# First block: the next stage starts from the un-normalised residual, and layer norm is applied to its results

## What is computed

```python
h = layer_norm(h, ln_in_g, ln_in_b)
for l in range(2):
    h = layer_norm(ALPHA * h + 0.5 * swiglu_ffn(h, ffn1...), ln_g[l,0], ln_b[l,0])
    mix = token_mix(h, ...)   # z = h @ w_in; pool, conv, retention; @ w_out
    h = layer_norm(ALPHA * h + mix, ln_g[l,1], ln_b[l,1])
    h = layer_norm(ALPHA * h + 0.5 * swiglu_ffn(h, ffn2...), ln_g[l,2], ln_b[l,2])
# layer_norm(x) = (x - mean) * rsqrt(var + eps) * g + b, over the 1024 features
```

## Time and profile before

| | |
|---|---|
| median of 3 runs | 1942.44 us (1942.26 to 1943.13) |
| span of the profiled execution | 1940.9 us |
| PE, PE weight load busy | 1769.2 us (91%), 1687.4 us (87%) |
| DVE, ACT, POOL busy | 1137.7, 816.8, 228.1 us |
| chain that ended last, by engine | PE 82%, DVE 9%, ACT 5%, issue 3% |

### The profile page before, as it was taken

How to read it: one execution, slowest core, us unless ns; L and a number is a source line. 1 busy time by engine, 2 the same in 40 slices (tenths; PEclk the granted TensorE clock), 3 DMA queues, 4 the chain that set the end, 5 groups by cost and what they waited for, 6 DMA issues and landing times.

```text
span 1940.9 us, 33661 instructions
## 1 busy us (share of the span) xinstructions
PE 1769.2 (91%) x13290; PEld 1687.4 (87%) x13290; DVE 1137.7 (59%) x1492; ACT 816.8 (42%) x1072; POOL 228.1 (12%) x258
## 2 busy tenths in 40 slices
PE   6999988889998999978889997899799978679998
PEld 5999987689998999978589996898799977579997
DVE  5555477665555555478665545566666456465654
ACT  4333353353334333254343334574434336543432
POOL 1000047000000000038010000130000001300000
PEclk9999999899999999999899999998899989789999
DMA  4545423134453445423144453242355523035552
GB/s 171 180 174 196 142 107 131 44 126 174 175 188 126 163 173 202 154 89 132 49 157 173 173 208 117 87 142 93 118 180 197 193 88 119 22 109 175 193 201 81
DMA packets 37096, 277.72 MB, mean 143 GB/s; under 512 B 4289, under 2 KB 4417, under 8 KB 6801
## 3 DMA queue, kind: packets, MB, share of 16 engines
q1 hardware_dynamic: 35872, 271.73, 39.6%
q0 software_dynamic: 1136, 4.83, 0.7%
HBM read 275.49 MB, written 1.05 MB: 142 GB/s over the span
## 4 chain that ended last, share of the span: by engine, by line
PE 82%; DVE 9%; ACT 5%; issue 3%; POOL 0%; DMA 0%; DVEq 0%; SPq 0%; ACTq 0%; POOLq 0%
PE bank L562 25%; PE bank L564 25%; PE bank L563 25%; PE bank L580 3%; DVE w_lo L1419 2%; DVE rstd L1427 1%; ACT w_hi L1015 1%; DVE conv_y L1580 1%; DVE o_rstd L1655 1%; DVE y L1439 1%; ACT h L1042 0%; ACT att_p L1221 0%; PE bank L823 0%; PE bank L849 0%; DMA ident<-in_ident 0%
## 5 line engine op out<-in xcount | busy, mean ns | idle before, releaser
L562 PE MATMUL bank<-h_hi,w_hi 128*128 128x272 f32 (+1 forms) x2624 | 763.3, 291 | 55.0 <-DVE h_lo L1443 26.7
L564 PE MATMUL bank<-h_hi,w_lo 128*128 128x272 f32 (+1 forms) x2624 | 760.7, 290 | 0.0
L563 PE MATMUL bank<-h_lo,w_hi 128*128 128x272 f32 (+1 forms) x2624 | 758.8, 289 | 0.0
L1419 DVE TENSOR_TENSOR w_lo<-raw,w_hi 128x2048 fp32r<-128x2048 f32 (+2 forms) x242 | 589.9, 2438 | 251.7 <-ACT w_hi L1015 250.3
L1015 ACT ACTIVATE w_hi<-raw 128x2048 fp32r<-128x2048 f32 (+2 forms) x241 | 486.2, 2018 | 221.3 <-PE bank L564 215.4
L562 PEld LDWEIGHTS bank<-h_hi,w_hi 128*128 128x128 f32 x2624 | 504.3, 192 | 61.5 <-issue 50.1
L564 PEld LDWEIGHTS bank<-h_hi,w_lo 128*128 128x128 f32 x2624 | 504.1, 192 | 0.0
L563 PEld LDWEIGHTS bank<-h_lo,w_hi 128*128 128x128 f32 x2624 | 503.9, 192 | 0.0
L562 PE MATMUL bank<-g_hi,w_hi 128*128 128x272 f32 (+1 forms) x1344 | 390.7, 291 | 7.7 <-DVE g_lo L1531 3.8
L564 PE MATMUL bank<-g_hi,w_lo 128*128 128x272 f32 (+1 forms) x1344 | 386.4, 287 | 0.0
L563 PE MATMUL bank<-g_lo,w_hi 128*128 128x272 f32 (+1 forms) x1344 | 385.6, 287 | 0.0
(11 more groups left out here) (249 smaller groups left out, 1411.1 us busy)
## 6 DMA issues: line engine op xcount, KB each, us to landing
raw<-in_up_w SPq DMA_DIRECT2D x132, 1024.0 KB, 4.7
raw<-in_down_w SPq DMA_DIRECT2D x48, 1408.0 KB, 6.0
raw<-in_in_w SPq DMA_DIRECT2D x20, 1024.0 KB, 4.7
raw<-in_out_w SPq DMA_DIRECT2D x16, 1024.0 KB, 4.8
raw<-in_even_w SPq DMA_DIRECT2D x12, 1024.0 KB, 4.8
raw<-in_odd_w SPq DMA_DIRECT2D x6, 1024.0 KB, 4.7
raw<-in_in_w SPq DMA_DIRECT2D x4, 512.0 KB, 3.4
decay<-in_decay POOLq DMA_DIRECT2D x1, 1632.0 KB, 10.9
```

The source lines that it names most:

```text
L562: pe.matmul(out, w[0], x[0], start=first, stop=False)
L563: pe.matmul(out, w[0], x[1], start=False, stop=False)
L564: return pe.matmul(out, w[1], x[0], start=False, stop=last)
L1419: dve.tensor_tensor(w_lo[:, slot, 0:blocks * P], raw[:, slot, 0:blocks * P], w_hi[:, slot, 0:blocks * P].bitcast(F32), ALU.subtract).then_ ...
```

## The change

**Five of the six layer norms of the first block are deferred** (all but the last, `LAST_NORM`). With r the residual tile, a constant per token m0 (the mean of tile 0) taken off it, and g, b the norm's gain and bias, the next stage's first chunks (4 up chunks, `DEFER_UP`, or 3 in-projection chunks, `DEFER_IN`) are multiplied from `u = g * r`, split as `u_hi`, `u_lo`. Two columns of u (274 instead of 272) hold -g and b, so that PE's result has -W g and W b beside it. DVE then turns a finished bank into `(bank + mu * (-Wg)) * rstd` (`deferred_norm`); the bias W b is added by ACT's silu or copy or by DVE. Meanwhile POOL normalises the residual itself in eight passes of 544 elements (`normalise`), ACT makes `h_hi` and `h`, DVE `h_lo`, and the chunks from `DEFER_UP` or `DEFER_IN` on use these as before.

**The statistics** come from two running sums on POOL, of y and of its squares (`residual_sums`), with one matmul by ones for each; variance is the mean square less the squared mean. POOL also takes m0 off the 7 or 6 tiles of `h` that are still to be added. The factor ALPHA is moved into the branch (`BRANCH_FFN`, `BRANCH_MIX`).

**The input norm** is taken token-wise on `x_tok` before the transposes (`bn_stats`), the constants' DMAs wait for x, and weight chunk 0 is loaded and split in two halves. **Order:** in the in-projection the pooling tiles come third (`IN_ORDER`), so `pool_windows` stands after the three deferred chunks; the first two taps on DVE stand later. The layer loop is written out twice.

The core of the diff (lines starting with a space are unchanged):

```diff
+IN_ORDER = [2, 3, 4, 5, 0, 1] + list(range(6, 22))
+BRANCH_FFN, BRANCH_MIX = 0.5 / ALPHA, 1.0 / ALPHA
+U = T + 2
+DEFER_UP, DEFER_IN = 4, 3
...
 # POOL
+            def residual_sums(taken):
+                pool.wait_ge(affine, seen.next(affine, KD))
+                pool.wait_ge(m0_copied, seen.next(m0_copied))
+                for k in range(taken, KD):
+                    pool.tensor_tensor(h[:, k, :], h[:, k, :], m0[:], ALU.subtract).then_inc(hm_ready, 1)
+                for k in range(1, KD):
...
+                    pool.tensor_tensor(acc[:], acc[:] if k > 1 else y[:, 0, :], y[:, k, :], ALU.add)\
...
+                    pool.tensor_tensor(acc2[:], acc2[:] if k > 1 else sqb[:, 0, :], sqb[:, k % 2, :], ALU.add)\
...
+            def normalise():
+                pool.wait_ge(u_ready, seen.next(u_ready, KD))
+                pool.wait_ge(mu_ready, seen.next(mu_ready))
+                pairs = [y[:, 2 * j:2 * j + 2, :] for j in range(KD // 2)]
+                for p in pairs:
+                    pool.tensor_tensor(p, p, both_tiles(mu), ALU.subtract).then_inc(t1_ready, 1)
+                pool.wait_ge(rstd_ready, seen.next(rstd_ready))
+                for p in pairs:
+                    pool.wait_ge(t1_ready, seen.next(t1_ready))
+                    pool.tensor_tensor(p, p, both_tiles(rstd), ALU.mult).then_inc(t_ready, 1)
...
 # PE
+            def shifted_tile(bank, slot, tiles, e, first):
+                for k in range(KD):
+                    if first:
+                        pe.wait_ge(u_ready, seen.next(u_ready))
+                    last = mm3(bank[:, 0:U], wpair(slot, k * tiles + e), upair(k), k == 0, k == KD - 1)
+                if first:
+                    residual_sums()
+                return last
...
 # ACT
+            def shifted_tile(l, i, k):
+                act.wait_ge(y_ready, seen.next(y_ready))
...
+                    act.activation(us(u_hi, k, 0, T), y[:, k, :], ACT.Identity, scale=vcol(l, V_LN + 16 * i + k))\
...
+                if k >= 2:
+                    act.wait_ge(acc2_added, seen.at(acc2_added, max(1, k - 2)))
+                act.activation(sqb[:, k % 2, :], y[:, k, :], ACT.Square).then_inc(squared, 1)
...
 # DVE
+            def residual_deviation():
+                dve.wait_ge(mean_ready, seen.next(mean_ready))
+                dve.tensor_scalar(mu[:], ps[6][:, 0:T], 1.0 / D, None, ALU.mult).then_inc(mu_ready, 1)
...
+            def deferred_norm(c, q, w, banks, free):
+                dve.wait_ge(chunk_used, st.value(c, 0, 2))
+                for e in range(2):
+                    last = dve.tensor_copy(wgb[:, w + e, :], banks[e][:, T:T + 2])
+                link(last)
+                for e in range(2):
+                    last = dve.scalar_tensor_tensor(q[:, e, :], mu[:], wgb[:, w + e, 0:1], banks[e][:, 0:T],
+                                                    ALU.mult, ALU.add)
...
+                dve.tensor_tensor(q, q, both_tiles(rstd), ALU.mult).then_inc(q_ready, 1)
...
+                def first_chunks():
+                    take(0)
+                    split_next(UP_BLOCKS, 0, 2)
+                    gated(0)
+                    take(1)
+                    split_next(UP_BLOCKS, 0, 3)
+                    low_tile(0)
...
+                    gated(1)
+                    take(2)
...
 # in-projection, DVE
-                    if c == 1:
-                        pool_windows()
...
+                take(0)
+                split_next(2 * KD, 0, 2)
+                take(1)
+                split_next(2 * KD, 0, 3)
...
+                dve.tensor_tensor(upad[:, :, TAPS - 1:], ca[:], cg[:], ALU.mult).then_inc(conv_in, 1)
+                for k in range(5):
+                    low_tile(k)
+                take(2)
+                split_next(2 * KD, 0, 4)
...
+                pool_windows()
```

More of the change, by code:

```diff
@@ L134, in region, with pairs_of @@
     return take
-def pairs_of(eng, n, step):
-    for j in range(2):
-        step(0, j, False)
-    with eng.Fori(1, n // 2 - 1) as i:
+def pairs_of(eng, n, step, done=2):
+    for c in range(done):
+        step(c // 2, c % 2, False)
+    with eng.Fori(done // 2, n // 2 - 1) as i:
         for j in range(2):
@@ L200, in forward @@
         spans = ((ghi_at + KD * T4, glo_at), (glo_at + KD * T4, g_end), (rest_at, limit))
-        one = placer(region(*spans))
+        late = placer(region((rest_at, limit)))
+        v_tok = late("v_tok", [P, 3, HEADS * P])
+        gate_s = late("gate_s", [P, HEADS, T])
+        o_c = late("o_c", [P, HEADS, T])
+        o_rstd = late("o_rstd", [P, HEADS, T])
+        late_end = rest_at + (3 * HEADS * P + 3 * HEADS * T) * 4
+        u_hi = place("u_hi", [P, KD * U], F32R, rest_at)
+        u_lo = place("u_lo", [P, KD * U], F32R, rest_at + KD * U * 4)
+        assert 2 * KD * U * 4 <= late_end - rest_at
+        one = placer(region((ghi_at + KD * T4, glo_at), (glo_at + KD * T4, g_end), (late_end, limit)))
         xpad = one("xpad", [P, 2, 16 + T])
@@ new lines, in forward @@
+        xstd_ready = sem("xstd_ready")
+        xscale_ready = sem("xscale_ready")
+        xn_ready = [sem(f"xn_ready{i}") for i in range(3)]
+        xT_ready = sem("xT_ready")
+        y_ready = sem("y_ready")
+        y0_ready = sem("y0_ready")
+        m0_ready = sem("m0_ready")
+        m0_copied = sem("m0_copied")
+        hm_ready = sem("hm_ready")
+        gb_done = sem("gb_done")
+        u_hi_done = sem("u_hi_done")
+        u_ready = sem("u_ready")
+        squared = sem("squared")
@@ L445, in ffn @@
                     src = a[name].rearrange("f c p n -> (f c) p n")
-                    with sp.Fori(0, n // 2) as c:
+                    ahead = 0
+                    if i == 0 and name == "up_w":
+                        half = UP_BLOCKS // 2 * P
+                        sp.dma_start(raw[:, 0, 0:half], src[0, :, 0:half]).then_inc(half_loaded, 16)
+                        sp.dma_start(raw[:, 0, half:2 * half], src[0, :, half:2 * half]).then_inc(loaded[0], 16)
+                        load(src[1], blocks, 1)
+                        ahead = 1
+                    with sp.Fori(ahead, n // 2) as c:
                         for j in range(2):
@@ L626, in down @@
                                    k == 0, k == FT - 1)
+                        if n == T and isinstance(i, int) and (i, j, k) == (0, 1, 3):
+                            shift()
                     last.then_inc(chunk_used, 1)
-                up(0, 0)
-                up(0, 1)
-                with pe.Fori(1, FT // 2) as i:
+                for c in range(shifted + 2):
+                    up(c // 2, c % 2, c)
+                with pe.Fori(shifted // 2 + 1, FT // 2) as i:
                     up(i, 0)
@@ L1556, in _ @@
+            for l in range(LAYERS):
+                ffn(IN_GROUPS[0] * KD, T, l, 0, l > 0)
+                split_next(IN_GROUPS[1] * KD, 0, 1)
+                residual_deviation()
                 dve.memset(xpad[:, :, 0:16], 0.0)
```

801 lines of the change are left out of this document (522 added, 279 removed).

## The result

The changed kernel runs in 1917.68 us (median of 4 runs, 1917.24 to 1924.63) beside 1942.79 us of the kernel before on the same chip: a ratio of 0.988 (95% interval 0.986 to 0.989). The forecast was 1908. The profiled execution has a span of 1915.4 us, 25.5 less than before, where 34 were forecast. All executions compared in this document are fast ones, except one of the four of b2 (3368.79 us), which its ratio leaves out.

A forecast was written before the change was run, and what follows sets the result against it. PE, with 82% of the chain of waits, was taken as the bound, so time is won only where it stands still. Terms -15 - 6.5 - 6 - 3 - 3.5 = -34 from 1942.4 gave 1908 us; range 1890 to 1927.

The forecast's parts named there:

- rivals 1 and 4: POOL and DVE exclude each other in full (1930 or 1924), or all five norms gain zero (1924); together 0.26.
- rival 1: POOL and DVE exclude each other in full: 1930 at all poor ends, else 1924; 0.26 shared with the zero-gain case.
- The start: Input norm and first chunk: chunk 0 starts at 20 to 21 us, -15 us (ends -13.5, -16.5).
- The norm behind the second feed-forward: Deferred norm in layer 0: 7.0 us lost where 13.5 were, so -6.5 us (ends -4.9, -8.9).
- The walk without POOL: Deferred norm before a feed-forward, POOL's passes left out: chunk 4 at 28.7 against 24.1 us, 4.6 us lost.
- the rows say less than in full: 0.1 us more: Deferred norm: DVE's two-input operation takes 537 ns beside the convolution, 442 elsewhere, so 7.0 us lost, not 8.6.
- The two out-projections: Norms behind them: 10.5 us lost where 13.5 were, -3 us each, -6 together (ends +1.8, -15.6).
- POOL comes late: Behind the out-projections: POOL's 20 operations, 17 us, start only 14.5 us before the last product.
- at no cost: Extra columns, down-stage drains, weight loads, constants and the written-out layer loop were said to cost nothing.
- In-projections: DVE bounds both: -6.7 to +3.6 us each, taken as -1.5 each, -3 together.
- The last norm: Not deferred, new statistics: squares at 16.3 us after the last product instead of 20.0, -3.5 us (-3 to -4).
- The table load: Root's load on the chain behind the square of mu: 1.28 us by its row, not the skill's 2.7.

The follow-up runs named there:

- b2: Changed kernel with PE's product for m0 issued four times in place of once, in all six stages with a residual: 1925.7 us, ratio 0.990.
- a1: Changed kernel with POOL's eight normalising passes cut from 2 x 272 to 2 x 8 elements in five deferred norms (result not the function's): 1895.8 us, ratio 0.974.
- b4: Changed kernel with each of POOL's eight normalising passes over two tiles cut into two passes over one: 1923.0 us, ratio 0.988.
- a2: Changed kernel with 18 of POOL's 20 m0 subtractions and running sums cut to 8 columns (result not the function's): 1916.1 us, ratio 0.984.
- a4: Changed kernel with DVE draining the first bank of an out-projection chunk ahead of the two u_lo of the chunk before: 1920.1 us, ratio 0.987.
- a3: Changed kernel with the nine table loads POOL issues in layer 1 put behind its normalising passes: 1917.1 us, ratio 0.985.
- b3: Changed kernel with POOL issuing the six constant loads at once, not only when x has landed: 1920.1 us, ratio 0.986.
- b1: Changed kernel with a one-column Sqrt on ACT ahead of its wait for mu, loading the root's table in idle time: 1919.0 us, ratio 0.985.
- c3: Changed kernel with rstd passes on DVE, table loads behind POOL's passes, early Sqrt, drain before u_lo, PE summing the last two squares: 1914.3 us, ratio 0.985.
- d1: As c3, with DVE's and ACT's work on the first chunks behind a feed-forward's deferred norm in another order: 1900.8 us, ratio 0.977.

## Why the prediction was right in sign and a quarter short

1917.7 us lies inside the range of 1890 to 1927, but at the upper end of the band of the forecast (1900 to 1917) and the lower end of the band of rivals 1 and 4 (1918 to 1931). The time alone doesn't tell the two apart; the stages do, and they show rival 1's mechanism behind the norms.

**The start** was right: -13.9 for -15. The statistics took 1.29 us per token group for the assumed 1.4, chunk 0 began at 19.34 for 20 to 21, and the 352nd triple ended at 154.1 for 153: PE's first 3.0 us held 5 triples, where its later pace has 8.

**The norm behind the second feed-forward** was right in the sum (-6.0 for -6.5), by luck: two errors cancel in part. The walk without POOL lost 4.6 us where a1 shows 3.4, and 2.4 us were put on POOL where it is 4.5. The step that failed is "the rows say less than in full: 0.1 us more", which set 7.0 between 4.6 and 8.6. A group's mean of 537 ns for 442 (rope beside the convolution) says nothing of what one operation pays when it meets a POOL operation on SBUF: 1.05 to 1.15 us for each of w_lo, gf, g_hi and g_lo. The 2.80 us addition of the earlier trace rows was the row to follow. Rival 1's mechanism was the true one there, and its price for the passes (8.6 - 4.6 = 4.0 us) is nearer to the 4.5 than the 2.4 taken. Its sign was there as well: POOL's rstd passes took 1.95 us on the mean, the mu passes, which meet less of DVE's work, 1.36. The Trainium skill (SBUF — State Buffer, Who interferes with whom) says that the two exclude each other for the whole instruction; a1 and b4 agree: without the passes w_lo takes 2.29 us, beside passes of 1.33 us 3.45, and beside halves 2.87. The same section of the Trainium skill names `tensor_scalar` among the operations that can take the ports shared with GpSimd, and the one-input g_hi, a `tensor_scalar`, did grow from 0.30 to 1.35 us; no run here shows in which mode it ran. The q of layer 1, which waited through several passes, goes beyond what the section says.

**The two out-projections** hold most of the miss: -2.2 and +1.7 us in place of -3 each. Two terms were mis-sized or missing. The drains inside the stage were put at 1 to 2.6 us and are 3.2 and 3.5; a2 and a4 share them out between POOL's backlog and DVE's u_lo ahead of the drain. The nine table loads stood in no term: "POOL comes late" counted its additions and not its DMA issues, and a3 prices them at 4.5 us. The 10.5 us taken held the norm and the drains together; measured they are 8.7 + 3.2 = 11.9 in layer 0 and 12.1 + 3.5 = 15.6 in layer 1, the latter with the 4.5 of the tables. The condition that I named for a wrong forecast, PE waiting more than 8 us for POOL, was just missed, and not as it was meant: PE waited 7.99 us up to 983.70 for a w_lo whose engine had waited for POOL.

**Down stages:** the product for m0 was missing from "at no cost"; it costs 0.4 us in each of four, 1.6 in all (b2: 0.45 for each further one). The drains there cost nothing, as said.

**In-projections:** -3.0 and +1.0 us for -1.5 each. In the seven profiles that leave it alone (the changed kernel and a2, a3, a4, b2, b3, with b4, which only halves its passes) the mean is 129.7 and 131.1 us, 2.1 under and 0.7 over the one profile of the kernel before: -1.4 us together where -3 was forecast, of the forecast's sign and half its size, and in layer 0 alone. PE waited for the convolution at 320.76, 99.7 us after the last product, inside the forecast 98 to 102. That DVE is the bound there fits PE's wait of 3.63 us for DVE's conv_y at 320.76 and a1, where 2.2 and 4.4 us came off with POOL's passes gone.

**The last norm** gave -4.6 for -3.5 (-3.5 to -5.0 over all the profiles). The squares started at 1189.34, 15.4 us after the last product ended, for 16.3 forecast; the 9.6 us from there are the same.

**The table load** was rightly taken at 1.28 us, and b1 shows that its 0.7 us on the chain is worth nothing while POOL's passes follow.

**Not in a stage:** the extra columns (on 864 matmuls, not 1088), the DMAs, the constants (b3) and the loop cost nothing that shows; the second block is 716.5 us in both.

## What to carry to other kernels

Work moved to an idle engine is not free if both engines then work on SBUF at once: price each operation of the critical engine that will meet it at one whole operation of the other at least, and count the other engine's DMA issues in its queue. A gap that goes leaves the next order of work exposed, and a fix may show nothing (the early root, the drain, the passes on DVE) until what stands behind it is mended too; the stage's own windows show this where the total does not. And after a cost has moved to a new engine, write its order anew by the times at which the waited-for engine needs each piece: here that was worth 13 us (c3 to d1), as much as the start.
